# The FFN's down projection as seven half-size block products instead of eight

## The reference, cut to what matters

```
    h = layer_norm(x) * (1 + sc2) + sh2
    gate, up = jnp.split(h @ w_ffn_up, 2, axis=-1)          # (1088, 1024) @ (1024, 5632)
    ffn = (jax.nn.silu(gate) * up) @ w_ffn_down              # (1088, 2816) @ (2816, 1024)
    x = layer_norm(ALPHA * x + (1 + g2) * ffn, ln2_g, ln2_b)
```

## Time and profile before

| what | value |
|---|---|
| time, three runs | 1451.94, 1453.12, 1454.38 us; median 1453.12 |
| the profiled execution, first to last instruction | 1453.1 us |
| TensorE busy | 1402.9 us (97%) |
| DVE, ACT, POOL busy | 898.0, 599.4, 491.7 us |
| down projection on TensorE | from 1177.1 to 1442.0 us |
| last matmul to the end | 11.1 us |

### The profile page before, as it was taken

One profiled execution on the slowest core, in us unless ns is written; L12 is line 12 of the kernel. 1 busy time (PEld: TensorE's weight loads), 2 busy tenths in 40 slices (PEclk: granted clock), 3 DMA queues, 4 the chain that ended last, 5 costly groups with the idle time before them and its releaser, 6 DMA issues.

```text
span 1453.1 us, 28832 instructions
## 1 busy us (share of the span) xinstructions
PE 1402.9 (97%) x10784; PEld 1269.7 (87%) x10784; DVE 898.0 (62%) x1486; ACT 599.4 (41%) x1431; POOL 491.7 (34%) x598
## 2 busy tenths in 40 slices
PE   6999899989899999999999999999999999999996
PEld 4799899988888888888799999999999988888664
DVE  5618796764457667787695555555545544665846
ACT  6524344436465666334633333233323333334241
POOL 3888866861133343322233212221221200000102
PEclk8999999999999999999999999999999999999999
DMA  9431434335545453522322222221222158576562
GB/s 328 127 104 47 113 99 123 107 84 159 157 144 181 132 163 113 180 90 79 95 61 82 82 75 75 73 88 60 81 81 84 36 192 276 174 251 233 182 224 74
DMA packets 159974, 185.59 MB, mean 128 GB/s; under 512 B 12732, under 2 KB 122112, under 8 KB 159872
## 3 DMA queue, kind: packets, MB, share of 16 engines
q1 hardware_dynamic: 156992, 172.49, 38.2%
q10 hardware_dynamic: 2880, 11.72, 2.1%
HBM read 147.23 MB, written 35.78 MB: 126 GB/s over the span
## 4 chain that ended last, share of the span: by engine, by line
PE 65%; DVE 4%; ACT 3%; issue 3%; POOL 1%; DMA 0%; POOLq 0%; ACTq 0%; DVEq 0%
PE bank L2155 29%; PE bank L2066 16%; PE bank L278 3%; PE bank L1651 2%; PE bank L1105 2%; PE bank L1114 2%; PE bank L1611 2%; PE bank L2074 1%; PE bank L1116 1%; ACT hp L1701 1%; PE bank L1147 1%; PE bank L1138 1%; DVE stat L1733 1%; ACT vp L1252 1%; DVE xt L1768 1%
## 5 line engine op out<-in xcount | busy, mean ns | idle before, releaser
L2155 PE MATMUL bank<-Tlo,rh 128*128 128x272 f32 x640 | 184.7, 289 | 0.0
L2155 PE MATMUL bank<-Thi,rh 128*128 128x272 f32 x640 | 184.2, 288 | 0.0
L2155 PE MATMUL bank<-Thi,rl 128*128 128x272 f32 x640 | 184.0, 288 | 0.0
L278 PE MATMUL bank<-hT_hi,whi 128*128 128x384 f32 (+1 forms) x504 | 167.8, 333 | 3.2 <-DVE wlo L268 1.9
L278 PE MATMUL bank<-hT_lo,whi 128*128 128x384 f32 (+1 forms) x504 | 165.9, 329 | 0.0
L278 PE MATMUL bank<-hT_hi,wlo 128*128 128x384 f32 (+1 forms) x504 | 165.8, 329 | 0.0
L2155 PE MATMUL bank<-hT_lo,rh 128*128 128x272 f32 x480 | 138.5, 289 | 0.0
L2155 PE MATMUL bank<-hT_hi,rl 128*128 128x272 f32 x480 | 138.4, 288 | 0.0
L2155 PE MATMUL bank<-hT_hi,rh 128*128 128x272 f32 x480 | 137.9, 287 | 0.0
L2010 POOL TENSOR_TENSOR sums<-raw 128x512 f32<-128x512 f32 x20 | 25.7, 1287 | 321.7 <-DVE rl L1896 303.9
L2155 PEld LDWEIGHTS bank<-Thi,rl 128*128 128x128 f32 x640 | 120.6, 188 | 0.0
(11 more groups left out here) (434 smaller groups left out, 3591.5 us busy)
## 6 DMA issues: line engine op xcount, KB each, us to landing
wd_raw<-w_down SPq DMA_DIRECT2D x52, 512.0 KB, 3.5
wada<-w_ada SPq DMA_DIRECT2D x12, 2048.0 KB, 9.3
raw<-w_up SPq DMA_DIRECT2D x40, 512.0 KB, 5.1
hid<-sil SPq DMA_DIRECT2D x40, 272.0 KB, 2.1
wraw<-w_in SPq DMA_DIRECT2D x21, 512.0 KB, 4.3
rows<-convrow ACTq DMA_DIRECT2D x16, 577.5 KB, 3.6
hid_raw<-hid SPq DMA_DIRECT2D x44, 192.0 KB, 3.6
wrx<-w_down SPq DMA_DIRECT2D x14, 512.0 KB, 3.5
```

Source lines behind the costliest of these rows:

```text
L278: last = nc.tensor.matmul(ps[banks[c]][:, 0:cw], w[:, slot, k * P:(k + 1) * P], a[:, k, c0:c0 + cw], start=(k == 0 and n == 0), stop=(k == ...
L2155: last = pe.matmul(ps[banks[c]][:, 0:NC], w[:, ks], a, start=(n < 3 and k == 0 and p == 0), stop=(k == 3 and p == 2), skip_group_check=True)
```

## The change

The eight full tiles (1024 tokens, two halves of 512), the 1024 output columns (two halves) and the 22 hidden blocks (two halves of 11, KH) are taken as a two by two block product, and its eight half-size products are replaced by seven, of sums of the blocks (Winograd's form). In the code's names the seven run in the order Q1, Q5, Q6, Q4, Q7, Q3, Q2. Each is 11 steps, so there are 77 steps, numbered 0 to 76: Q6 is steps 22 to 32, Q4 33 to 43, Q7 44 to 54, Q3 55 to 65, Q2 66 to 76. A step has one 128x512 piece of weights and one 128x512 piece of hidden values, and TensorE does 4 tiles times 3 = 12 matmuls of 512 columns.

What comes with it:

- **Sums of operands.** In Q5, Q6, Q4 and Q7 the weight piece is a difference that POOL makes (`sum_w`, 44 of them). In Q5, Q6, Q7 and Q3 the hidden piece is a sum or difference that DVE makes (`sum_h`, 44), ahead of the two `lo` parts of a step (`down_lo`).
- **Sums of products.** ACT copies the products Q1 and Q5 out of PSUM (`keep_product`), DVE adds Q6 and then Q4 to them (`second_u`, `fourth_u`, `less_p4`), POOL multiplies the parts by the gate row and adds them to x1 (`scale_p1`, `scale_v`, `right_of_A`, `scale_u`, `left_of_A`, `rest_of_A`, `half_of_B`). Q7 ends tiles 4 to 7, Q3 the right half of tiles 0 to 3, and Q2 their left half.
- **Banks.** Products go round seven PSUM banks, four a product. So the fourth tile of a product waits (`bank_free`) for the first bank of the product before it to be read: by ACT behind its splits of step 15 or 26, by DVE behind its splits of step 37, 48, 59, or 70.
- **Loads.** Each piece is 256 KB. SP issues them in one fixed order on eight semaphores; the weights that Q7 needs again are fetched (`b12_again`) once the split of the same buffer in Q4 is done.
- **The half tile** is spread over Q1, Q5, Q7 and Q3, one hidden block ahead of a step, with the hidden values of the sample tokens in one buffer (`hsam`).
- **The norm's scale and shift** are ACT's and POOL's for seven of the nine tiles (`PASS2`).
- The last six steps (71 to 76) are ordered by tile.

```diff
-        TAIL = (FB - 3, FB - 3, FB - 5)
-        ENDS = (0, 1, 2, 3, 4, 5, 8, 6, 7)
-        PASS2 = (TILES - 3, TILES - 2)
-        SPLITS = 6
-        dw_hi = [wd_hi[:, n, :] for n in range(4)] + [wdx[:, n, :] for n in range(2)]
-        dw_lo = [wd_lo[:, n, :] for n in range(4)] + [wdx[:, n, :] for n in range(2, 4)]
-        dh_hi = [hid_hi[:, n, :] for n in range(4)] + [hidx[:, n, :] for n in range(2)]
-        dh_lo = [hid_lo[:, n, :] for n in range(4)] + [hidx[:, n, :] for n in range(2, 4)]
...
+        KH = FB // 2
+        RING = len(slots)
+        ROT = (3, 4, 0, 1, 6, 7, 2)
+        HALF_BANK = 5
+        ENDS = (4, 5, 6, 7, 8, 0, 1, 2, 3)
+        PASS2 = (0, 1, 2, 3, 4, 6, 7)
+        Q1, Q5, Q6, Q4, Q7, Q3, Q2 = range(7)
+        STEPS = 7 * KH
+        LAST = STEPS - RING
+        down_bank = lambda q, r: ROT[(4 * q + r) % 7]
+        w_hi_of = lambda s: slots[s % RING][:, 0, :]
+        w_lo_of = lambda s: slots[s % RING][:, 1, :]
+        h_hi_of = lambda s: slots[s % RING][:, 2, :]
+        h_lo_of = lambda s: slots[s % RING][:, 3, :]
...
+        H_SUMS, W_SUMS = (Q5, Q6, Q7, Q3), (Q5, Q6, Q4, Q7)
...
+        for k in range(KH):
+            IN += [("A", Q1, k), ("W", Q1, k)]
+            IN += [("hsam", 0, 0)] if k == 5 else []
+            IN += [("B", Q5, k - 6)] if k > 5 else []
+            IN += [("S", Q5, k - 7)] if k > 6 else []
+        for k in range(KH):
+            IN += [("S", Q5, 4 + k)] if 4 + k < KH else []
+            IN += [("A", Q5, k)]
+            IN += [("B", Q5, 5 + k)] if 5 + k < KH else []
+        for k in range(KH):
+            IN += [("A", Q6, k), ("B", Q6, k)]
+            IN += [("x1", 0, k // 2 - 1)] if k in (2, 4, 6, 8) else []
+            IN += [(("g2", "ln2")[k // 4], 0, k % 4 // 2)] if k in (1, 3, 5, 7) else []
+        for k in range(KH):
+            IN += [("A", Q4, k), ("B", Q4, k)] + ([("W", Q7, k - 2)] if k > 1 else [])
...
+                def b12_again(k):
+                    sp.wait_ge(on["d_lo"], since("d_lo", Q4 * KH + k + 1))
+                    fetch(("W", Q7, k), tq[k][:], wd_rows(k, 1))
+                for k in range(KH):
+                    load_a(Q4, k, KH + k, 1)
+                    load_b(Q4, k, KH + k, 0)
+                    if k > 1:
+                        b12_again(k - 2)
+                for k in range(KH):
+                    if k < 2:
+                        b12_again(KH - 2 + k)
+                    load_a(Q7, k, k, 0)
+                    load_a(Q7, k, k, 1, 1)
+                    load_b(Q7, k, KH + k, 1)
...
+            def sum_w(q, k):
+                if q == Q5:
+                    landed(pool, "W", Q1, k)
+                    landed(pool, "B", q, k)
+                    pool.wait_ge(on["d_lo"], since("d_lo", Q1 * KH + k + 1))
+                    pool.wait_ge(on["f_half"], since("f_half", k + 1))
+                    x, y = raw_b(q, k), tq[k]
+                elif q == Q6:
+                    landed(pool, "B", q, k)
+                    pool.wait_ge(on["d_lo"], since("d_lo", Q5 * KH + k + 1))
+                    x, y = raw_b(q, k), tq[k]
+                elif q == Q4:
+                    landed(pool, "B", q, k)
+                    pool.wait_ge(on["d_lo"], since("d_lo", Q6 * KH + k + 1))
+                    x, y = tq[k], raw_b(q, k)
+                else:
+                    landed(pool, "B", q, k)
+                    landed(pool, "W", q, k)
+                    x, y = raw_b(q, k), tq[k]
+                pool.tensor_tensor(tq[k][:], x[:], y[:], ALU.subtract).then_inc(on["w_sum"], 1)
...
+            def scale_p1(r):
+                pool.wait_ge(on["p_read"], since("p_read", r + 1))
+                g(pool.tensor_tensor(p1acc[:, r, :], p1acc[:, r, :], g2r[:, 0, h0], ALU.mult))
+            def scale_v(r):
+                pool.wait_ge(on["u_sum"], since("u_sum", r + 1))
+                g(pool.tensor_tensor(vacc[:, r, :], vacc[:, r, :], g2r[:, 0, h1], ALU.mult))
+            def right_of_A(r):
+                landed(pool, "x1", 0, r)
+                g(pool.tensor_tensor(accA[r][:, h1], accA[r][:, h1], vacc[:, r, :], ALU.add))
...
+            for k in range(KH):
+                sum_w(Q5, k)
+            for k in range(KH):
+                sum_w(Q6, k)
+            for n, c in ((DEC_SEQ, 1), (P, 0)):
+                landed(pool, "g2", 0, c)
+                pool.tensor_scalar(g2r[0:n, c, :], g2r[0:n, c, :], 1.0, 1.0 / ALPHA, ALU.add, ALU.mult).then_inc(on["f_g2"], 1)
+            pool.wait_ge(on["f_g2"], since("f_g2", 2))
+            for k in range(KH):
+                sum_w(Q4, k)
+                if k > 5:
+                    scale_p1(k - 6) if k < 10 else scale_v(0)
+            for k in range(KH):
+                sum_w(Q7, k)
+                if k < 3:
+                    scale_v(k + 1)
+                elif k < 7:
+                    right_of_A(k - 3)
+                else:
+                    scale_u(k - 7)
+            for r in range(4):
+                left_of_A(r)
+            rest_of_A(0)
...
+            def bank_free(q, r):
+                n = 4 * q + r
+                if n in (2, 3):
                     pe.wait_ge(on["st_sil"], since("st_sil", (FB - 3) * 4 + 2))
-                elif t == 2:
+                elif n in (4, 5):
                     pe.wait_ge(on["st_u"], since("st_u", (FB - 3) * 10 + 8))
-                elif t == 3:
+                elif n == 6:
                     pe.wait_ge(on["st_u"], since("st_u", (FB - 2) * 10))
-                elif t > 3:
-                    pe.wait_ge(on["f_tmp"], 2 * (t - 4) + 2)
-            def products(t, h, k):
-                n, sl = tile_rows(t), (g * FB + k) % SPLITS
-                cols = slice((t % 3) * P, (t % 3) * P + n)
-                for m, (a, w) in enumerate(((dh_hi, dw_hi), (dh_hi, dw_lo), (dh_lo, dw_hi))):
-                    last = pe.matmul(ps[DBANKS[t % 4][h]][0:n, :], a[sl][:, cols], w[sl][:, h * 512:(h + 1) * 512],
-                                     start=(k == 0 and m == 0), stop=(k == FB - 1 and m == 2))
+                elif 7 <= n < 15:
+                    pe.wait_ge(on["p_kept"], since("p_kept", n - 7 + 1))
+                elif n >= 15:
+                    pe.wait_ge(on["p_read"], since("p_read", n - 7 - 8 + 1))
...
+            def products(q, k, r):
+                s = q * KH + k
+                rows = slice(r * P, (r + 1) * P)
+                for m, (a, w) in enumerate(((h_hi_of(s), w_hi_of(s)), (h_hi_of(s), w_lo_of(s)), (h_lo_of(s), w_hi_of(s)))):
+                    last = pe.matmul(ps[down_bank(q, r)][:], a[:, rows], w, start=(k == 0 and m == 0), stop=(k == KH - 1 and m == 2))
                 return last
...
+            for q in range(7):
+                for k in range(KH):
+                    s = q * KH + k
+                    if q == Q1 and k > 5:
+                        half_tile(k - 6)
+                    if q == Q5 and k + 5 < KH:
+                        half_tile(k + 5)
+                    if q == Q7 and k > 7:
+                        half_tile(KH + k - 8)
+                    if q == Q3 and k + 3 < KH:
+                        half_tile(KH + k + 3)
+                    if s >= LAST:
+                        break
+                    step_in(s)
+                    for r in range(4):
+                        if k == 0:
+                            bank_free(q, r)
+                        last = products(q, k, r)
+                        if k == KH - 1:
+                            last.then_inc(on["f_tile"], 1)
+                    if k < KH - 1:
+                        last.then_inc(on["f_dn"], 1)
+            for r in range(4):
+                for s in range(LAST, STEPS):
+                    if r == 0:
+                        step_in(s)
+                    last = products(Q2, s - Q2 * KH, r)
+                last.then_inc(on["f_tile"], 1)
...
+            if s >= RING:
+                slot_free(act, s - RING)
+            if q == Q1:
+                landed(act, "W", q, k)
+            elif q in W_SUMS:
+                act.wait_ge(on["w_sum"], since("w_sum", w_sum_at(q, k)))
+            else:
+                landed(act, "B", q, k)
+            act.activation(w_hi_of(s), w_raw(q, k), ACT.Copy).then_inc(on["d_hi"], 1)
+            if q in H_SUMS:
+                act.wait_ge(on["h_sum"], since("h_sum", h_sum_at(q, k)))
+            else:
+                landed(act, "A", q, k)
+            act.activation(h_hi_of(s), h_raw(q, k), ACT.Copy).then_inc(on["f_hi"], 1)
...
+            for s in range(AHEAD, STEPS):
+                down_hi(act, s)
+                if s in ((Q1 + 1) * KH + 4, (Q5 + 1) * KH + 4):
+                    for r in range(4):
+                        keep_product(act, s // KH - 1, r)
...
+            def second_u(r):
+                dve.wait_ge(on["p_kept"], since("p_kept", r + 1))
+                dve.tensor_tensor(uacc[:, r, :], p1acc[:, r, :], made(Q6, r), ALU.add).then_inc(on["p_read"], 1)
+            def fourth_u(r):
```

(99 more changed lines are left out.)

527 lines of the change are left out of this document (304 added, 223 removed).

## The result

The changed kernel takes 1478.16 us (median of 4 runs, 1477.1 to 1479.12) against 1452.72 us of the kernel before: ratio 1.0178, 95% interval 1.0164 to 1.0191. It is 25 us slower; forecast were 1474 us, with 1442 to 1488 as the range. The profiled execution spans 1475.1 us from its first to its last instruction; its own time is 1477.1. In every run that lists both, the time is 1.7 to 2.2 us above the span of its execution, and the sum behind the forecast was one of the span.

What follows compares the result with a forecast made beforehand. TensorE bounded the kernel before; after the change DVE and POOL, taking turns at SBUF, would make it wait. Terms: 1413.3 + 5 + 20 + 8 + 10 + 3 = 1459.3, and 14: about 1474 us, range 1442 to 1488.

Steps and rivals of the forecast that it cites:

- stream without stalls ends: Down projection: TensorE's 236.2 us of matmuls and half-tile blocks, started at 1177.1, would end at 1413.3 us without waits.
- a) into Q6, step 22: Into Q6, POOL's 13 turns in a row delay DVE by 16 us; TensorE waits 5 us at step 22, bounds 0 and 10.
- b) Q4 and Q7, step 44: Q4 and Q7: late loads and DVE's 15 instructions, each a turn, make TensorE wait 20 us together, bounds 4 and 27.
- c) step 66: Q3 into Q2: TensorE waits at step 66 for a read behind step 70's split; late by 3 to 13, taken as 8 us.
- d) the last six splits: Last six steps, ordered by tile: DVE and POOL need 29.5 us against TensorE's 15; 10 us of waiting, bounds 2 and 14.
- clock: TensorE at half clock after four long waits, 1.7 us lost each: 0 to 7 us, taken as 3.
- behind the last matmul: The end: DVE's statistics and four tiles, POOL's shifts and the store take 13 to 14 us instead of 11.1.
- The matmuls: Down projection: 77 steps of 12 matmuls, 924, 132 fewer at 0.2266 us each, 29.9 us less; a step 2.72 us.
- The turns: DVE instructions with two SBUF operands and reading POOL instructions alternate, one each; a turn of both costs 1.70 us.
- transfers on top: Rival, chance 0.12: a 256 KB piece takes 3.5 us, not 2.7; Q7's start and Q4's loads wait longer: 1480 us.
- The cover holds: Rival, chance 0.14: POOL's work falls into DVE's gaps, or DVE keeps its rate beside it: 1431.5 us.
- Half of the waits: Rival, chance 0.12: POOL's own waits keep its bursts short, so waits b, c and d halve: 1452 us.

Runs made afterwards that it cites:

- Experiments 1 to 3: Changed kernel with POOL's 44 weight sums on 8 columns: 1461.68 us; its gate, residual and shift work on 8 columns instead: 1454.33 us; both: 1436.25 us.
- experiment 3: Changed kernel with POOL's weight sums and its gate, residual and shift operations all on 8 columns, every instruction and wait kept: 1436.25 us, ratio 0.9874 to the kernel before.
- experiment 5: Changed kernel with POOL's 44 weight sums replaced by fills of a constant over the same 512 columns: 1459.33 us, ratio 1.0038 to the kernel before.
- experiment 4: Changed kernel with Q7's last two refetched weight pieces loaded behind its fourth and fifth step's loads, not ahead of its first: 1472.78 us, ratio 1.0118 to the kernel before.
- experiment 9: Changed kernel with weight sums on DVE, gate work cut and moved to DVE, late Q7 refetch, fewer POOL shifts, DVE work reordered: 1452.78 us, ratio 0.9996 to the kernel before.

## Why the prediction was right

By its own terms, from the distances between matmuls in the profiled execution:

| term | forecast | measured |
|---|---|---|
| stream without stalls ends | 1413.3 | 1413.8 (start 1176.5, half tile 24 us, and 3.7 in small distances) |
| a) into Q6, step 22 | 5 | 3.6, and 1.7 in Q5 |
| b) Q4 and Q7, step 44 | 20 | 3.4 and 18.8 |
| c) step 66 | 8 | 6.6 |
| d) the last six splits | 10 | 5.3 |
| clock | 3 | 9.4 |
| behind the last matmul | 14 | 12.3 |
| end | 1473 to 1474 | 1475.1 |

Against the median time of 1478.16 us the forecast of 1474 was 4 us low. Under 2 us of that are in the terms; the rest is that a time is some 2 us longer than its span, which the forecast left out.

**The matmuls.** 924, at the old price: 12 of them and a half-tile block took 3.96 us in Q7 (1364.52 to 1368.48), of which the twelve are 2.72 by the price of the earlier trace rows.

**The turns** were the step on which all rested. Their price (1.67 against 1.70 us), their condition (two SBUF operands against a reading POOL) and their places (steps 22, 44 and 66, fourth tile each, then the last six) came out as read in the earlier trace rows. Experiments 1 to 3 and 5 show the cause: with the same DVE instructions in the same order and nearly nothing for POOL to read, the time is 42 us shorter (experiment 3), and with the 44 sums as writes alone 19 us shorter (experiment 5).

**Mis-sized.** The clock: I took one stretch of 3.4 us behind each wait and thought the splits would hide it. The records show half clock in four stretches of the stream, and some 45 matmul distances in them cost 9.4 us in all. The terms add up to 1462.6 us, and the last matmul ends at 1462.8. The last six splits overlapped with TensorE more than I gave them (5.3, not 10). With the 1.7 us too many behind the last matmul this cancels the 6.4 us too few of the clock: that the sum comes within 2 us of the span is in part luck. The pieces of 256 KB landed in 4.2 to 4.4 us in the two largest groups and not in 2.7 (3.9 and 5.4 in the two smaller ones):

```profile
rA<-hid SPq DMA_DIRECT2D x84, 256.0 KB, 4.4
rB<-w_down SPq DMA_DIRECT2D x77, 256.0 KB, 4.2
```

ACT waited 38.8 us for pieces of w_down (21.8 in the waits above, and 17.0 for the `tq` pieces of Q1), but none of the waits of TensorE's matmuls is put down to a transfer, and experiment 3 has the same transfers and takes 1436 us: the rival *transfers on top* is out as a cause of its own. Of it stays that 4 to 5 us of term b were the loads' order (experiment 4). The term had two waits of 2.5 for it; ahead of steps 43 and 44 TensorE waited 1.3 and 2.1 us.

**The other rivals.** *The cover holds* would have been 1431.5; experiment 3, without turns, took 1436, so that sum was near, and its condition was what failed. *Half of the waits*, 1452: in Q7 POOL's row was unbroken over ten turns, and waits a and c came near their full size.

**Left open.** How much of the 9.4 us would have been lost to late splits without the fall of the clock: no kernel here changed the clock alone. Open too is how much of the 42 us of experiment 3 comes from POOL delivering its results sooner, outside the wait of step 44.

## What to carry to other kernels

Work put on an idle GpSimd is not free if it reads SBUF beside a VectorE that is fed from SBUF: add its time, less what it waits, to VectorE's, and compare the sum with the bound engine stage by stage; here it cost 42 us, against 30 us of saved matmuls. Moving such work to VectorE one for one gained little here (0.94 for 0.80 us). Cutting it gained more (experiment 9), and beside reads of PSUM or as pure writes it cost VectorE nothing (experiment 5). And a product scheme with fewer matmuls ends with more sums on the tail: look at what is left behind the last matmul before counting the gain.

## What the runs showed of the hardware that was not expected

- The turns hold over a long row, where the earlier trace rows had two or three: ten in a row in Q7, 1.67 us each, and neither engine got two instructions running.
- A POOL fill of 128x512 takes 0.53 us, a sum of the same size 1.29 alone, and the fill costs DVE nothing.
- POOL's smallest operation on a column of one (line 2238) takes 0.22 us at 1457.89, started ahead of DVE's instruction, and 1.21 at 1463.25, where it ends just behind a DVE instruction of 1024 columns that was under way: it waits its turn as well.
- The clock was half for 3.4 us behind a distance of 3.9 us between two matmuls (step 22), for 10 us from 1441.6 on, around three distances of 1.4 to 2.7 us with matmuls between, and in experiment 4 for 3.4 us behind one of 2.6 us. Behind the distances of 1.9 us in Q5, and of 1.6 and 2.3 us ahead of steps 43 and 44, it stayed full.
